# Moving the matmul operands of a three-block transformer kernel to other SBUF addresses

## The chip, the cores and the metric

The kernel runs on one core of one Trainium2 chip. The metric is the device time of one execution in microseconds; a change is judged by the median of several runs against the median of the kernel before on the same chip.

## The reference, cut to what matters

Three transformer blocks are computed one behind the other for 256 tokens of width 1024, all in float32. Block A mixes with dilated band attention in three head groups, block B with ordinary causal attention, block C with a forgetting attention beside a convolution and a pooling branch. Each block ends in a gated MLP of hidden width 2816:

```
x = x + mixer(rmsnorm(x)) @ w_o          # A, B, C: three kinds of mixer
u = rmsnorm(x) @ w_up                     # 1024 -> 2 x 2816
gate, val = split(causal_conv3(u))
x = x + (silu(gate) * val) @ w_down       # 2816 -> 1024
```

## The kernel before, in words

Activations lie transposed, 128 channels on the partitions and 256 tokens along the row. The weights stream from HBM in chunks of 128 x 1024 values through a ring of six buffers `w_raw`. A float32 product is made of three products of a faster float type (`fp32r`): every operand is split into a high part and a low rest, and hi·hi, hi·lo and lo·hi are added in PSUM. ScalarE makes the high part of a weight chunk (`w_hi`), VectorE the rest (`w_lo`); the same is done for the activations (`xg` with a high and a low half for each 128 channels, the attention result `mix_hi`/`mix_lo`, the gated product `g_hi`/`g_lo`).

TensorE runs one list of matmuls in the order of the code, and four patterns make up nearly all of its time. Every matmul is preceded by the load of its 128 x 128 stationary tile, which runs beside the matmul ahead of it.

- **Up-projection pair** (`project2_k`, L417 and L419, 352 pairs in each of the three MLPs): stationary `w_hi`, moving 512 columns (high and low half of `xg` together); then stationary `w_lo`, moving the 256 columns of the high half.
- **Down-projection triple** (L1747 to L1749, 176 triples in each MLP): stationary `w_hi` with `g_hi` moving, `w_hi` with `g_lo`, `w_lo` with `g_hi`, 256 columns each.
- **Out-projection triple** (`out_pe`, L1223 to L1225, 64 triples in each block): the same three with `mix_hi` and `mix_lo`. Block C's six extra projections (L403 to L405, 48 triples) do the same with `xg`.
- **QKV triple** (L665 to L667, 556 triples over the three blocks, and 60 more matmuls of the same shape in L599): here `xg` is stationary and 384 columns of weights move: `w_hi` past the high half of x, `w_lo` past the high half, `w_hi` past the low half.

The SBUF tensors are laid one behind the other in the order in which they are made. The rest of this text speaks of an operand's **residue**: its start address in bytes modulo 128. All steps between the tiles of one tensor (512, 1024, 2048 bytes) are multiples of 128, so that a tensor's tiles have one residue. Two small dummy tensors and three tables set them:

```python
SHIFT = 32
X_AT = (0, 0, 0, 8, 0, 16)              # floats; attention A, MLP A, attention B, MLP B, ...
G_AT = ((0, 0), (8, 8), (24, 24))       # MLP A, B, C: g_hi, g_lo; the tensor starts at residue 32
MIX_AT = ((0, 0), (8, 8), (16, 16))     # attention A, B, C: mix_hi, mix_lo
...
    sb("w_gap", [P, 16])
    w_lo = [sb(f"w_lo{s}", [P, CHUNK], F32R) for s in range(RING)]
    sb("x_gap", [P, 16])
```

```python
    def project2_k(eng, c, e, b, k):
        s = c % RING
        nc.tensor.matmul(bank(b, 0, 2 * TOK), w_hi[s][:, k * P:(k + 1) * P], xg[e][:, k, :, :].rearrange("p h t -> p (h t)"),
                         start=(k == 0), stop=False, skip_group_check=True)
        last = nc.tensor.matmul(bank(b), w_lo[s][:, k * P:(k + 1) * P], xg_hi[e][:, k, :], start=False,
                                stop=(k == KT - 1), skip_group_check=True)
```

The second argument of `matmul` is the stationary tile, the third the moving one.

Of the kernel before, what the change touches and what calls it, by code (L numbers as in the profile page):

```python
# [8 lines left out]
P = 128  # L9
D = 1024  # L10
TOK = 256
KT = D // P
# [27 lines left out]
WARM_UP = 16  # L40
HALVES = 3
GAINS = 16
X0 = 224
GAP = 184
SHIFT = 32
X_AT = (0, 0, 0, 8, 0, 16)
G_AT = ((0, 0), (8, 8), (24, 24))
MIX_AT = ((0, 0), (8, 8), (16, 16))
CHUNK = KT * P
UNIT = 3 * P  # L50
QCHUNK = 2 * UNIT
# [112 lines left out]
def build(nc, x_d, xa_d, stream_d, par_d, con_d, taps_d, out_d):  # L164
    F32 = mybir.dt.float32
    F32R = mybir.dt.float32r
# [5 lines left out]
    def sb(name, shape, dt=F32):  # L172
        return nc.alloc_sbuf_tensor(name, shape, dt)

    def sem(name):
# [2 lines left out]

    w_raw = [sb(f"w_raw{s}", [P, CHUNK]) for s in range(RING)]
    w_hi = [sb(f"w_hi{s}", [P, CHUNK], F32R) for s in range(RING)]  # L180
    sb("w_gap", [P, 16])
    w_lo = [sb(f"w_lo{s}", [P, CHUNK], F32R) for s in range(RING)]
    sb("x_gap", [P, 16])
    x_all = sb("x_all", [P, X0 + KT * TOK])
    xT = x_all[:, X0:X0 + KT * TOK].rearrange("p (k t) -> p k t", t=TOK)
    xg_all = sb("xg", [P, KT * 2 * TOK + SHIFT], F32R)
    xg = [xg_all[:, o:o + KT * 2 * TOK].rearrange("p (k h t) -> p k h t", h=2, t=TOK) for o in X_AT]
    xg_hi, xg_lo = [x[:, :, 0, :] for x in xg], [x[:, :, 1, :] for x in xg]
    mix_all = [sb(f"mix_{n}", [P, KT * TOK + SHIFT], F32R) for n in ("hi", "lo")]
    mix_hi, mix_lo = [[mix_all[n][:, o[n]:o[n] + KT * TOK].rearrange("p (k t) -> p k t", t=TOK) for o in MIX_AT]  # L190
                      for n in range(2)]
    par = sb("par", [P, N_PAR])
    con = sb("con", [P, N_CON])
    zero = sb("zero", [P, TOK], BF16)
    sb("gap", [P, GAP - 3 * SHIFT])
    ln_x = sb("ln_x", [P, TOK])
    rms_r = sb("rms_r", [P, TOK])

# [30 lines left out]
    g_all = sb("g_hi0", [P, 4 * TOK + SHIFT], F32R)  # L229
    g_hi, g_lo = [[[g_all[:, o[n] + (2 * n + b) * TOK:o[n] + (2 * n + b + 1) * TOK] for b in range(2)] for o in G_AT]  # L230
                  for n in range(2)]
# [219 lines left out]
    def norm_gain(e, m):  # L451

        g = PAR_NORM + KT * e + m
        return x_all[:, X0 - GAINS + m:X0 - GAINS + m + 1] if e == 0 else par[:, g:g + 1]

# [1640 lines left out]
    with nc.Block() as block:  # L2096

        @block.sync
        def _(sp):
# [9 lines left out]
            def load_x(m, n, landed):  # L2109
                a, b = GAINS + m * TOK if m else 0, GAINS + (m + n) * TOK  # L2110
                sp.dma_start(x_all[:, X0 - GAINS + a:X0 - GAINS + b], xa_d[:, a:b]).then_inc(landed, 16)

# [297 lines left out]
```

## Time and profile before

| | us |
|---|---|
| median of 3 runs (1051.97 to 1052.17) | 1052.13 |
| the profiled execution | 1052.06 |
| its span, first to last instruction | 1050.2 |
| TensorE busy in it | 1045.3 |
| VectorE, ScalarE, GpSimd busy | 864.6, 686.9, 346.6 |

The 1.9 us between the execution and its span lie around the program. TensorE's matmuls overlap (the drain of one lies over the start of the next), so the length that the trace gives to one matmul is not what it costs; that is the step from its start to the start of the next, which is read from a list of instructions in order of time. Divided over many steps, its 0.01 us of resolution is enough.

### The profile page before, as it was taken

What the parts mean: (1) busy time and instruction counts of PE and PEld (TensorE: products, weight loads), DVE (VectorE), ACT (ScalarE), POOL (GpSimd) and SP (SyncE); (2) the same over time, 40 slices, a digit from 0 to 9 for tenths busy, and PEclk for the clock granted to TensorE, in tenths of its full rate; (3) what the DMA queues carried; (4) which work ended last, traced back from release to release, by engine and by line L of the source; (5) the groups of instructions that cost most, each with busy time, mean ns of one, the idle gap of its engine ahead of it and who ended that gap; (6) DMA issues with size and microseconds to landing.
All of it is one profiled execution on the core that took longest, in us unless ns stands there. A gap on an engine that the chain in (4) does not pass through costs nothing.

```text
span 1050.2 us, 21191 instructions
## 1 busy us (share of the span) xinstructions
PE 1045.3 (100%) x7496; PEld 974.4 (93%) x7496; DVE 864.6 (82%) x1589; ACT 686.9 (65%) x1264; POOL 346.6 (33%) x370
## 2 busy tenths in 40 slices
PE   9999999999999999999999999999999999999998
PEld 8999999999999999999989899999998998999998
DVE  7877778777799888887776999888896769998886
ACT  7766776766766555576776766555686667666563
POOL 4312222112355333332121564333341015653331
PEclk9999999999999999999999999999999999999999
DMA  8644455456466555535453666555433436665541
GB/s 312 235 159 152 156 162 169 149 170 205 159 218 216 189 183 195 166 101 185 152 181 122 200 205 200 192 184 181 153 114 135 161 121 201 209 210 183 196 161 41
DMA packets 57749, 183.34 MB, mean 175 GB/s; under 512 B 6352, under 2 KB 9680, under 8 KB 57424
## 3 DMA queue, kind: packets, MB, share of 16 engines
q1 hardware_dynamic: 56816, 181.52, 52.1%
q10 hardware_dynamic: 864, 0.92, 0.3%
q8 instruction: 41, 0.67, 0.2%
q14 instruction: 28, 0.23, 0.1%
HBM read 181.36 MB, written 1.05 MB: 174 GB/s over the span
## 4 chain that ended last, share of the span: by engine, by line
PE 99%; DMA 0%; DVE 0%; ACT 0%; DVEq 0%; issue 0%
PE ps L417 23%; PE ps L419 12%; PE ps L665 10%; PE ps L667 9%; PE ps L666 9%; PE ps L1747 6%; PE ps L1749 6%; PE ps L1748 6%; PE ps L1223 2%; PE ps L1225 2%; PE ps L1224 2%; PE ps L599 1%; PE ps L843 1%; PE ps L888 1%; PE ps L817 1%; PE ps L855 1%
## 5 line engine op out<-in xcount | busy, mean ns | idle before, releaser
L385 DVE TENSOR_TENSOR w_lo<-w_raw,w_hi 128x1024 fp32r<-128x1024 f32 (+2 forms) x369 | 442.4, 1214 | 45.8 <-ACT w_hi L377 45.5
L377 ACT ACTIVATE w_hi<-w_raw 128x1024 fp32r<-128x1024 f32 (+2 forms) x369 | 353.7, 972 | 150.2 <-PE ps L419 125.2
L417 PE MATMUL ps<-xg,w_hi 128*128 128x512 f32 x1056 | 369.6, 393 | 0.0
L419 PE MATMUL ps<-xg,w_lo 128*128 128x256 f32 x1056 | 294.6, 279 | 0.0
L417 PEld LDWEIGHTS ps<-xg,w_hi 128*128 128x128 f32 x1056 | 198.4, 188 | 41.7 <-DVE xg L482 0.2
L419 PEld LDWEIGHTS ps<-xg,w_lo 128*128 128x128 f32 x1056 | 198.9, 188 | 0.1
L1869 POOL TENSOR_TENSOR prob_t<-prob_t,qkT 128x256 f32<-128x256 f32 x63 | 102.1, 1621 | 279.1 <-ACT prob_t L1792 279.1
L665 PE MATMUL ps<-w_hi,xg 128*128 128x384 f32 (+1 forms) x556 | 193.4, 348 | 0.0
L667 PE MATMUL ps<-w_hi,xg 128*128 128x384 f32 (+1 forms) x556 | 187.6, 337 | 0.0
L666 PE MATMUL ps<-w_lo,xg 128*128 128x384 f32 (+1 forms) x556 | 186.6, 336 | 0.0
L1749 PE MATMUL ps<-g_hi,w_lo 128*128 128x256 f32 x528 | 148.2, 281 | 0.0
L1747 PE MATMUL ps<-g_hi,w_hi 128*128 128x256 f32 x528 | 147.6, 279 | 0.0
L1748 PE MATMUL ps<-g_hi,w_hi 128*128 128x256 f32 x528 | 147.1, 279 | 0.0
L1863 POOL TENSOR_TENSOR qkT<-prob,rms_r 128x256 f32<-128x256 f32 x132 | 121.2, 937 | 18.7 <-DVE prob L1806 13.5
L1839 DVE SCALAR_TENSOR_TENSOR qkT<-qkT,par 128x255 f32<-128x255 f32 (+1 forms) x264 | 111.8, 475 | 5.3 <-ACT qkT L1785 5.2
L665 PEld LDWEIGHTS ps<-w_hi,xg 128*128 128x128 f32 x556 | 104.6, 188 | 3.3 <-issue 2.7
L1785 ACT ACTIVATE qkT<-qkT,par 128x256 f32<-128x256 f32 x132 | 77.6, 597 | 42.4 <-POOL qkT L1863 41.5
L666 PEld LDWEIGHTS ps<-w_lo,xg 128*128 128x128 f32 x556 | 104.5, 188 | 0.1
L667 PEld LDWEIGHTS ps<-w_hi,xg 128*128 128x128 f32 x556 | 104.3, 188 | 0.0
L1747 PEld LDWEIGHTS ps<-g_hi,w_hi 128*128 128x128 f32 x528 | 99.8, 189 | 3.1 <-issue 0.8
L1748 PEld LDWEIGHTS ps<-g_hi,w_hi 128*128 128x128 f32 x528 | 99.1, 188 | 0.0
L1749 PEld LDWEIGHTS ps<-g_hi,w_lo 128*128 128x128 f32 x528 | 99.0, 188 | 0.0
(191 smaller groups left out, 1385.8 us busy)
## 6 DMA issues: line engine op xcount, KB each, us to landing
w_raw<-w_stream SPq DMA_DIRECT2D x228, 512.0 KB, 3.6
w_raw<-w_stream SPq DMA_DIRECT2D x137, 384.0 KB, 3.3
w_raw<-w_stream SPq DMA_DIRECT2D x4, 392.0 KB, 3.0
con<-consts SPq DMA_DIRECT2D x1, 1024.0 KB, 7.6
x_all<-x_t SPq DMA_DIRECT2D x4, 256.0 KB, 5.3
conv_taps<-taps SPq DMA_DIRECT2D x1, 1024.0 KB, 7.4
w_raw<-w_stream SPq DMA_DIRECT2D x4, 192.0 KB, 4.6
x_all<-x_a SPq DMA_DIRECT2D x3, 256.0 KB, 5.7
```

The lines of the kernel that those rows point to most:

```text
L377: nc.scalar.activation(w_hi[s][:, 0:w], w_raw[s][:, 0:w], ACT.Copy).then_inc(w_hi_done, 1)
L385: nc.vector.tensor_tensor(w_lo[s][:, 0:w], w_raw[s][:, 0:w], w_hi[s][:, 0:w].bitcast(F32), ALU.subtract).then_inc(w_lo_done, 1)
L417: nc.tensor.matmul(bank(b, 0, 2 * TOK), w_hi[s][:, k * P:(k + 1) * P], xg[e][:, k, :, :].rearrange("p h t -> p (h t)"), start=(k == 0), st ...
L419: last = nc.tensor.matmul(bank(b), w_lo[s][:, k * P:(k + 1) * P], xg_hi[e][:, k, :], start=False, stop=(k == KT - 1), skip_group_check=True)
L665: nc.tensor.matmul(out, hi, wh, start=(k == 0), stop=False)
L666: nc.tensor.matmul(out, hi, wl, start=False, stop=False)
L667: last = nc.tensor.matmul(out, lo, wh, start=False, stop=(k == KT - 1))
L1747: nc.tensor.matmul(acc(m), wh, g_hi[f][b], start=first, stop=False, skip_group_check=True)
L1748: nc.tensor.matmul(acc(m), wh, g_lo[f][b], start=False, stop=False, skip_group_check=True)
L1749: last = nc.tensor.matmul(acc(m), wl, g_hi[f][b], start=False, stop=True, skip_group_check=True)
L1839: nc.vector.scalar_tensor_tensor(cv_s[b][s][:, k:TOK], up_s[b][s][:, 0:TOK - k], par_col(f, t, per, i, 4 * s + 2 - k), cv_s[b][s][:, k:TOK ...
L1863: nc.gpsimd.tensor_tensor(up_s[t % 2][s], up_sum[s], rms_r[:], ALU.mult).then_inc(F.up, 1)
```

## The change

Only addresses change: no instruction is added, removed or moved on any engine, and no wait. The two dummy tensors go, so that `w_lo` starts at a multiple of 128 bytes as `w_hi` does. X0 grows by as many floats as they had, so that x itself stays where it was. The three tables get other offsets, `mix_hi` and `mix_lo` become 32 floats longer, and a dummy behind them gets shorter by as much, so that all that follows stays where it was; the parameters and constants between move by 256 bytes.

```diff
-X0 = 224
+X0 = 256
-X_AT = (0, 0, 0, 8, 0, 16)
-G_AT = ((0, 0), (8, 8), (24, 24))
-MIX_AT = ((0, 0), (8, 8), (16, 16))
+X_AT = (24, 16, 8, 24, 24, 8)
+G_AT = ((8, 8), (0, 0), (0, 0))
+MIX_AT = ((48, 48), (16, 16), (56, 56))
...
-    sb("w_gap", [P, 16])
-    sb("x_gap", [P, 16])
-    mix_all = [sb(f"mix_{n}", [P, KT * TOK + SHIFT], F32R) for n in ("hi", "lo")]
+    mix_all = [sb(f"mix_{n}", [P, KT * TOK + 2 * SHIFT], F32R) for n in ("hi", "lo")]
-    sb("gap", [P, GAP - 3 * SHIFT])
+    sb("gap", [P, GAP - 5 * SHIFT])
```

The residues that follow, in bytes modulo 128, in the order of blocks A, B, C:

| operand | before | after |
|---|---|---|
| `w_hi` | 0 | 0 |
| `w_lo` | 64 | 0 |
| `xg` in attention | 0, 0, 0 | 96, 32, 96 |
| `xg` in the MLP | 0, 32, 64 | 64, 96, 32 |
| `g_hi`, `g_lo` | 32, 64, 0 | 64, 32, 32 |
| `mix_hi`, `mix_lo` | 0, 32, 64 | 64, 64, 96 |

## Rows read from the trace of the kernel before

**Rows 1.** The page: span, busy time of the engines, chain that ended last

```profile
span 1050.2 us, 21191 instructions
...
PE 1045.3 (100%) x7496; PEld 974.4 (93%) x7496; DVE 864.6 (82%) x1589; ACT 686.9 (65%) x1264; POOL 346.6 (33%) x370
...
PE 99%; DMA 0%; DVE 0%; ACT 0%; DVEq 0%; issue 0%
```

**Rows 2.** MLPs A, B, C: length, busy by engine, granted clock, DMA share, GB/s

```profile
276.79:461.76 184.97, 184.96 (x1236) 170.44 (x1235) 165.32 (x235) 114.31 (x172) 76.43 (x69) 1.00 0.55 184
575.69:761.98 186.29, 186.29 (x1236) 170.52 (x1235) 166.09 (x234) 114.99 (x171) 76.88 (x70) 1.00 0.56 186
863.97:1050.20 186.23, 183.03 (x1236) 168.14 (x1234) 165.13 (x235) 109.08 (x162) 79.41 (x70) 1.00 0.51 169
```

**Rows 3.** TensorE in order of time: up-projection pairs; start us, length us, line

```profile
350.03 0.39 PE L417 MATMUL ps<-xg,w_hi 128*128 128x512 f32 x1
...
352.45 0.39 PE L417 MATMUL ps<-xg,w_hi 128*128 128x512 f32 x1
...
639.82 0.40 PE L417 MATMUL ps<-xg,w_hi 128*128 128x512 f32 x1
...
643.31 0.39 PE L417 MATMUL ps<-xg,w_hi 128*128 128x512 f32 x1
...
950.83 0.39 PE L417 MATMUL ps<-xg,w_hi 128*128 128x512 f32 x1
...
952.53 0.39 PE L417 MATMUL ps<-xg,w_hi 128*128 128x512 f32 x1
...
870.55 0.40 PE L417 MATMUL ps<-xg,w_hi 128*128 128x512 f32 x1
...
874.40 0.40 PE L417 MATMUL ps<-xg,w_hi 128*128 128x512 f32 x1
```

**Rows 4.** The same list: first down-projection matmul, and the pair that follows

```profile
352.80 0.28 PE L1747 MATMUL ps<-g_hi,w_hi 128*128 128x256 f32 x1
...
355.63 0.39 PE L417 MATMUL ps<-xg,w_hi 128*128 128x512 f32 x1
...
643.65 0.28 PE L1747 MATMUL ps<-g_hi,w_hi 128*128 128x256 f32 x1
...
646.49 0.40 PE L417 MATMUL ps<-xg,w_hi 128*128 128x512 f32 x1
...
949.78 0.28 PE L1747 MATMUL ps<-g_hi,w_hi 128*128 128x256 f32 x1
...
950.48 0.40 PE L417 MATMUL ps<-xg,w_hi 128*128 128x512 f32 x1
```

**Rows 5.** The same list: out-projections of blocks A, B, C, second matmul of triples

```profile
254.22 0.28 PE L1224 MATMUL ps<-mix_lo,w_hi 128*128 128x256 f32 x1
...
260.87 0.28 PE L1224 MATMUL ps<-mix_lo,w_hi 128*128 128x256 f32 x1
...
559.90 0.28 PE L1224 MATMUL ps<-mix_lo,w_hi 128*128 128x256 f32 x1
...
565.24 0.28 PE L1224 MATMUL ps<-mix_lo,w_hi 128*128 128x256 f32 x1
...
848.55 0.28 PE L1224 MATMUL ps<-mix_lo,w_hi 128*128 128x256 f32 x1
...
853.75 0.28 PE L1224 MATMUL ps<-mix_lo,w_hi 128*128 128x256 f32 x1
```

**Rows 6.** The same list: QKV triples of block A, and the first chunks (L599)

```profile
132.04 0.34 PE L665 MATMUL ps<-w_hi,xg 128*128 128x384 f32 x1
...
135.17 0.34 PE L665 MATMUL ps<-w_hi,xg 128*128 128x384 f32 x1
...
7.20 1.20 PE L599 MATMUL ps<-w_hi,xg 128*128 128x384 f32 x6
8.24 0.50 PE L599 MATMUL ps<-w_lo,xg 128*128 128x384 f32 x2
```

## Prediction, on record before the changed kernel ran

> **What bounds the kernel now.** I read the page first. TensorE is busy for 1045.3 of 1050.2 us and holds 99% of the chain that ended last [rows 1], so time is won or lost only where a matmul starts earlier or later after the one ahead of it. The granted clock is 1.00 in all three MLPs [rows 2], that is 2.4 GHz, so a slower clock is not the reserve. VectorE, the next engine, is busy for 165 to 166 us of the 185 to 186 us of an MLP [rows 2]: some 19 us of slack in each.
>
> Then I compared the three MLPs with each other. They run the same 1236 matmuls and differ in little but addresses: TensorE is busy in them for 184.96, 186.29 and 183.03 us [rows 2]. The spread of 3.3 us is what addresses (and a few waits) are worth in one MLP, and it has a place: the step from matmul to matmul.
>
> - A pair of the up-projection, 512 + 256 = 768 columns, takes 2.42 us / 7 = 345.7 ns in MLP A, 3.49 / 10 = 349 ns in B, and 1.70 / 5 = 340 ns in C; but at its beginning C runs pairs of 3.85 / 11 = 350 ns on the very same addresses [rows 3].
> - A triple of the down-projection, also 768 columns, takes 2.83 / 8 = 354 ns in A, 2.84 / 8 = 355 ns in B, 0.70 / 2 = 350 ns in C [rows 4].
> - A triple of the out-projection takes 6.65 / 19 = 350 ns in block A, 5.34 / 15 = 356 ns in B, 5.20 / 15 = 346.7 ns in C [rows 5].
> - A QKV triple (1152 columns) takes 3.13 / 6 = 521.7 ns [rows 6].
>
> The best, 340 ns for 768 columns, is 0.443 ns a column; I call that the floor (a QKV triple: 510 ns). What lies above it is the reserve that addresses may hold: per pair 6, 9 and about 2 ns (C's mix of its two rhythms, taken as 342), per down triple 14, 15 and 10, per out triple 10, 16 and 7, per QKV triple 12. With 352 pairs, 176 down triples and 64 out triples a block, and 556 QKV triples, that is 17 x 0.352 + 39 x 0.176 + 33 x 0.064 + 12 x 0.556 = 6.0 + 6.9 + 2.1 + 6.7 = 21.7 us in all.
>
> **A reading of the rows.** While one matmul streams its moving tile, the stationary tile of the next is read. I call the **distance** the residue of the moving tile minus that of the stationary tile being loaded. Before, `w_lo` stood 64 off `w_hi`, so the distance alternated: pairs 64, 0 in A, 96, 32 in B, 0, 64 in C; down triples 32, 96, 32 in A, 64, 0, 64 in B, 0, 64, 0 in C; out triples 0, 64, 0 in A, 32, 96, 32 in B, 64, 0, 64 in C; QKV 0, 64, 0. Odd multiples of 32 are slow where they occur (B's pairs 349, B's out triples 356, A's down triples 354), but the pattern 64, 0, 64 gives 355 in one place and 346.7 in another, and C's pairs show two rhythms. So residues set what is possible, and the rhythm that the engine falls into decides some 8 to 10 ns of it. That is the uncertainty of all that follows.
>
> After the change the distance is constant in every pattern: pairs 64, 96, 32; down triples 64, 32, 32; out triples 64, 64, 96; QKV 32, 96, 32. The trace has one long enough run of constant distance: the six L599 matmuls on `w_hi` (distance 0) take 1.04 / 6 = 173.3 ns each, 520 a triple against 521.7 with the alternating distance [rows 6]. Against the floor of 510 that is 10 instead of 11.7 ns, 15% of the excess gone. No row shows a constant distance of 32, 64 or 96.
>
> **The change part by part**, on the profiled execution of 1052.06 us (the median of the runs is 0.07 above it).
>
> 1. *Pairs.* A's x moves to C's present residue, 64: I give it C's mix, 342 ns, −3.7 ns x 352 = −1.3 us. B (96) and C (32) have no row; I give them the mean of the four measured rhythms, (345.7 + 349 + 340 + 350) / 4 = 346.2: B −2.8 ns, −1.0 us, C +4.2 ns, +1.5 us. Sum −0.8. Bounds: all at 340 is −17 x 0.352 = −6.0; all at 350 is (4.3 + 1 + 8) x 0.352 = +4.7.
> 2. *Down triples.* The mean of the six measured triples is 352; with 15% of the 12 ns of excess gone, 350: −4, −5 and 0 ns x 176 = −1.6 us. Bounds: all at 340 −6.9, all at 356 (2 + 1 + 6) x 0.176 = +1.6.
> 3. *Out triples.* A and B go to 64, where C stands now: 346.7, −3.3 and −9.3 ns; C goes to 96, between 346.7 and 356: 351, +4.3. Sum −8.3 x 0.064 = −0.5 us, between −2.1 and +1.0 (all at 356). The 48 triples of L403 to L405 I leave at zero: 9 ns, the spread of the out triples, would be 0.4 us either way.
> 4. *QKV triples.* The constant run's 520: −1.7 ns x 556 = −0.9 us. Lower bound the floor, −6.5 (11.7 ns). Upper bound: out triples have 16 ns of excess at odd distances against 10 at even ones; the same ratio makes 11.7 ns to 18.7, +7 x 0.556 = +3.9.
> 5. *The other engines.* VectorE writes `w_lo`, and VectorE and ScalarE write `xg`, `g` and `mix` at other residues; the weights land where they did. I put this at nothing: a slower subtraction is covered by the 19 us of slack per MLP, and would cost only above it. The chain has no visible share of VectorE or ScalarE [rows 1]. A shorter or longer step on TensorE also doesn't move the weight stream much: its DMA engines are busy for 51 to 56% [rows 2].
>
> Sum: −0.8 − 1.6 − 0.5 − 0.9 = −3.8 us, **1048.3 us**.
>
> **Rivals.**
>
> *Slower: odd distances are the bad ones.* Nearly all new positions are 32 or 96 away: two of three MLPs in pairs and down triples, C's out-projection, all QKV. In the rows B's pairs and out triples, at 32 and 96, are the slowest of their kind, and A's down triples are slower than C's. Price: pairs at the slow rhythm of 350 +4.7; down triples of B and C at 356 +1.2; out C +0.6 and A, B −0.8; QKV +3.9: +9.6, 1061.7 us. It begins to decide where QKV alone goes up by more than 7 ns a triple, since that eats the whole forecast. With half of it the time is about 1057. Against it: before, 32 and 96 came mixed, and constant they have no row.
>
> *No change, 1052.1 us.* Either TensorE's two reads do not meet, or gains and losses cancel (A's pairs −1.3 against C's +1.5 shows how easily). For the first half speaks nothing in the rows: the same matmuls take 183.03 to 186.29 us [rows 2]. On this the Trainium skill (SBUF — State Buffer, Who interferes with whom) says that TensorE has independent read ports for the moving tile and for the load of the stationary one and never waits on anyone; by that rule residues would be worth nothing and the time would stay at 1052.1, which the three MLPs' spread contradicts unless something else causes it.
>
> *A large gain.* If a constant distance lets the engine fall into the 340 rhythm everywhere, as C's MLP does for most of its pairs, all 21.7 us go: 1030.4. For it: C's pairs hold that rhythm through whole chunks [rows 3]. Against it: the one constant run stays 10 ns above the floor [rows 6]. Half of it is 1041.
>
> **How the numbers follow.** A measurement of this kernel tells about 0.2% (2.1 us) from no change. Forecast, between 1040 and 1050: 0.40. Large gain, below 1040: 0.08. No change, 1050 to 1054.2: 0.20. Slower: 0.32, of which a third, 0.10, above 1058. So faster 0.48, same 0.20, slower 0.32, and the range 1040 to 1058 leaves 0.18 out. Since cases of both signs hold most of the chance: the forecast's own range is 1040 to 1050.
>
> **What would show it.** Same counts of matmuls and a granted clock of 1.00 on both sides; TensorE busy about 183, 184 and 184 us in the three MLPs; pairs near 342 ns in MLP A and 346 in B and C; down triples near 350; QKV triples near 520, out triples of A and B near 347. The forecast is wrong if QKV triples rise above 525, if pairs settle at 350 in two MLPs, or if VectorE's subtraction for `w_lo` gets so much longer that waits for it appear in the chain.

## The result: slower by 0.23%

The changed kernel took 1054.51 us (median of 10 runs, 1054.29 to 1055.85) against 1052.14 us of the kernel before on the same chip: a ratio of 1.0023, 95% interval 1.0014 to 1.0032. The forecast was 1048.3 us in a range of its own from 1040 to 1050. The time lies outside that, on the other side of no change, and still within the wider 1040 to 1058; by the limits of the prediction it is a slower kernel (above 1054.2), which had a chance of 0.32.

The same lines of the page as in [rows 1] (span, busy time of the engines, chain):

```profile
span 1052.6 us, 21191 instructions
...
PE 1047.9 (100%) x7496; PEld 975.5 (93%) x7496; DVE 863.6 (82%) x1589; ACT 686.3 (65%) x1264; POOL 345.2 (33%) x370
...
PE 99%; DMA 0%; DVE 0%; ACT 0%; DVEq 0%; issue 0%
```

The count of instructions and the chain are the same, and TensorE is busy for 2.6 us longer (1047.9 against 1045.3). VectorE takes 1 us less. So the time was lost where the forecast looked for a gain, in the steps of TensorE. The three MLPs, after the change (from and to, length, busy time of TensorE, weight loads, VectorE, ScalarE, GpSimd; granted clock, DMA share, GB/s), beside [rows 2]:

```profile
275.82:462.67 186.85, 186.85 (x1236) 170.80 (x1235) 165.02 (x235) 113.86 (x172) 76.37 (x69) 1.00 0.56 182
576.01:761.99 185.98, 185.98 (x1237) 170.01 (x1235) 166.24 (x234) 115.05 (x171) 77.18 (x70) 1.00 0.58 186
864.81:1052.57 187.76, 184.51 (x1236) 170.11 (x1234) 164.28 (x235) 108.83 (x162) 77.64 (x69) 1.00 0.52 168
```

TensorE's busy time went from 184.96 to 186.85 us in A, from 186.29 to 185.98 in B and from 183.03 to 184.51 in C: +1.9, −0.3, +1.5. The granted clock is 1.00 in all of them, the 2.4 GHz of before.

What a pair and a down triple cost after the change is read from one chunk of each MLP: start of 16 pairs, start of the 8 triples behind them, start of the next pairs (start us, length us, line; L415 is what L417 was, L1745 what L1747 was). They answer to [rows 3, 4]:

```profile
312.80 0.40 PE L415 MATMUL ps<-xg,w_hi 128*128 128x512 f32 x1
...
318.46 0.28 PE L1745 MATMUL ps<-g_hi,w_hi 128*128 128x256 f32 x1
...
321.28 0.40 PE L415 MATMUL ps<-xg,w_hi 128*128 128x512 f32 x1
...
613.08 0.39 PE L415 MATMUL ps<-xg,w_hi 128*128 128x512 f32 x1
...
618.68 0.28 PE L1745 MATMUL ps<-g_hi,w_hi 128*128 128x256 f32 x1
...
621.51 0.39 PE L415 MATMUL ps<-xg,w_hi 128*128 128x512 f32 x1
...
901.70 0.39 PE L415 MATMUL ps<-xg,w_hi 128*128 128x512 f32 x1
...
907.25 0.28 PE L1745 MATMUL ps<-g_hi,w_hi 128*128 128x256 f32 x1
...
910.05 0.39 PE L415 MATMUL ps<-xg,w_hi 128*128 128x512 f32 x1
```

A pair takes 5.66 / 16 = 354 ns in A, 5.60 / 16 = 350 in B, 5.55 / 16 = 347 in C; a down triple 2.82 / 8 = 352.5, 2.83 / 8 = 354 and 2.80 / 8 = 350 ns. The out-projections of blocks A, B and C (first matmul of triples 18, 14 and 14 steps apart), as in [rows 5], and QKV triples of block A, 14 steps apart, as in [rows 6]:

```profile
253.38 0.28 PE L1221 MATMUL ps<-mix_hi,w_hi 128*128 128x256 f32 x1
...
259.74 0.28 PE L1221 MATMUL ps<-mix_hi,w_hi 128*128 128x256 f32 x1
...
560.82 0.28 PE L1221 MATMUL ps<-mix_hi,w_hi 128*128 128x256 f32 x1
...
565.58 0.28 PE L1221 MATMUL ps<-mix_hi,w_hi 128*128 128x256 f32 x1
...
849.13 0.28 PE L1221 MATMUL ps<-mix_hi,w_hi 128*128 128x256 f32 x1
...
854.17 0.28 PE L1221 MATMUL ps<-mix_hi,w_hi 128*128 128x256 f32 x1
```

```profile
100.78 0.34 PE L663 MATMUL ps<-w_hi,xg 128*128 128x384 f32 x1
...
108.06 0.34 PE L663 MATMUL ps<-w_hi,xg 128*128 128x384 f32 x1
```

Out triples take 6.36 / 18 = 353 ns in A, 4.76 / 14 = 340 in B and 5.04 / 14 = 360 in C; a QKV triple takes 7.28 / 14 = 520. The 340 of block B does not hold for its whole stage. After a wait it runs differently, 16 triples in 5.65 us, which is 353 ns:

```profile
569.30 0.28 PE L1221 MATMUL ps<-mix_hi,w_hi 128*128 128x256 f32 x1
...
574.95 0.28 PE L1221 MATMUL ps<-mix_hi,w_hi 128*128 128x256 f32 x1
```

From here on a step is given as the mean over its whole stage, worked out from all starts in the trace; steps more than 4.5% above the stage's median, which hold a wait, are left out on both sides (1 or 2 in 100 in pairs and down triples, 9 to 14 in out triples, 12 to 21 in QKV triples, a third in block C's extra projections). Steps in ns, with what each term of the forecast became:

| term | before A, B, C | after A, B, C | forecast us | measured us |
|---|---|---|---|---|
| pairs (352 an MLP) | 346.7, 350.7, 341.9 | 352.5, 350.1, 346.7 | −0.8 | +3.5 |
| down triples (176) | 353.4, 353.9, 350.1 | 353.5, 353.3, 350.0 | −1.6 | −0.1 |
| out triples (64) | 351.7, 355.7, 347.0 | 353.3, 347.0, 359.8 | −0.5 | +0.4 |
| block C's extra projections (48) | 353.7 | 359.6 | 0 | +0.3 |
| QKV triples (556) | 523.5, 523.0, 526.3 | 519.9, 521.9, 524.0 | −0.9 | −1.6 |
| sum | | | −3.8 | +2.5 |

Each measured term is the sum of the step differences times the counts; their sum of +2.5 us stands beside +2.3 us in the spans (1052.57 against 1050.23) and +2.4 us in the medians. So all of the loss is in these steps. The pairs lose 3.5 us, which is more than the whole; the out triples and the extra projections lose 0.7, and the QKV and down triples give back 1.7. Of block C's QKV triples a quarter move 392 columns instead of 384, and take 534 to 535 ns before and after, so the mean of C stands above those of A and B for that reason alone: its triples of 384 columns are at 523.4 and 520.0 ns.

### The profile page after: what moved, and what is told of

It reads as the page before. It is cut to its first block, busy times and chain, and to the rows that moved or that the text cites. A ratio compares the mean times of both kernels' runs of the same rounds, so it can differ in the third digit from the quotient of the medians.

```text
span 1052.6 us, 21191 instructions
## 1 busy us (share of the span) xinstructions
PE 1047.9 (100%) x7496; PEld 975.5 (93%) x7496; DVE 863.6 (82%) x1589; ACT 686.3 (65%) x1264; POOL 345.2 (33%) x370
## 4 chain that ended last, share of the span: by engine, by line
PE 99%; DMA 0%; DVE 0%; ACT 0%; DVEq 0%; issue 0%
PE ps L415 23%; PE ps L417 12%; PE ps L663 10%; PE ps L664 9%; PE ps L665 9%; PE ps L1745 6%; PE ps L1746 6%; PE ps L1747 6%; PE ps L1221 2%; PE ps L1222 2%; PE ps L1223 2%; PE ps L597 1%; PE ps L841 1%; PE ps L886 1%; PE ps L815 1%; PE ps L853 1%
## 5 line engine op out<-in xcount | busy, mean ns | idle before, releaser
L375 ACT ACTIVATE w_hi<-w_raw 128x1024 fp32r<-128x1024 f32 (+2 forms) x369 | 353.9, 972 | 155.9 <-PE ps L417 130.7
L415 PE MATMUL ps<-xg,w_hi 128*128 128x512 f32 x1056 | 372.7, 393 | 0.0
L417 PE MATMUL ps<-xg,w_lo 128*128 128x256 f32 x1056 | 296.6, 281 | 0.0
L415 PEld LDWEIGHTS ps<-xg,w_hi 128*128 128x128 f32 x1056 | 198.2, 188 | 43.0
L417 PEld LDWEIGHTS ps<-xg,w_lo 128*128 128x128 f32 x1056 | 198.6, 188 | 0.1
L1747 PE MATMUL ps<-g_hi,w_lo 128*128 128x256 f32 x528 | 147.5, 279 | 0.0
L1745 PE MATMUL ps<-g_hi,w_hi 128*128 128x256 f32 x528 | 147.5, 279 | 0.0
L1745 PEld LDWEIGHTS ps<-g_hi,w_hi 128*128 128x128 f32 x528 | 99.2, 188 | 3.1 <-issue 0.3
L1747 PEld LDWEIGHTS ps<-g_hi,w_lo 128*128 128x128 f32 x528 | 99.2, 188 | 0.0
```

Source lines behind the costliest of these rows:

```text
L375: nc.scalar.activation(w_hi[s][:, 0:w], w_raw[s][:, 0:w], ACT.Copy).then_inc(w_hi_done, 1)
L1745: nc.tensor.matmul(acc(m), wh, g_hi[f][b], start=first, stop=False, skip_group_check=True)
L1747: last = nc.tensor.matmul(acc(m), wl, g_hi[f][b], start=False, stop=True, skip_group_check=True)
```

## The experiments

Three questions: do addresses alone decide a step, and is it the distance between two tiles that counts; with what period; and what decides between several steps at the same addresses. In the first four expectations, theory D says that the distance modulo 128 decides alone, theory R that it sets bounds and the state in which TensorE enters a chunk decides some 10 ns of it. Residues are given modulo 256 from here on: `w_hi` stands at 128; `w_lo` at 192 before and at 128 after; x at 128 plus four times its table entry.

### Either half of the change alone

`w_lo` moved, x, gated product and mixed heads where they were before (against the changed kernel):

```diff
-X_AT = (24, 16, 8, 24, 24, 8)
-G_AT = ((8, 8), (0, 0), (0, 0))
-MIX_AT = ((48, 48), (16, 16), (56, 56))
+X_AT = (0, 0, 0, 8, 0, 16)
+G_AT = ((0, 0), (8, 8), (24, 24))
+MIX_AT = ((0, 0), (8, 8), (16, 16))
```

> One part of the change alone: the low weights at residue 0, the three tables as before. Theory D (a pattern's step follows from the distances of moving and next stationary tile, taken modulo 128, wherever it stands): QKV at constant distance 0 runs at the 520 ns a triple that the six L599 matmuls of before showed; the pairs of MLP B (distance 32, 32) run at the 346.7 ns that MLP C shows after the change, the pairs of MLP C (64, 64) at the 352.5 ns that MLP A shows after the change; the down triples of B (64) at 353.5. With MLP A at 0, 0 unknown that is about 1052 to 1055 us. Theory R (distances only bound it, the rhythm in which a pattern is entered decides within some 10 ns): the same distances give other steps, by 3 to 10 ns, in at least one of these places.

The other half: `w_lo` left at 192, the tables of the change (against the kernel before; `mix` is longer and `gap` shorter, as in the change):

```diff
-X_AT = (0, 0, 0, 8, 0, 16)
-G_AT = ((0, 0), (8, 8), (24, 24))
-MIX_AT = ((0, 0), (8, 8), (16, 16))
+X_AT = (24, 16, 8, 24, 24, 8)
+G_AT = ((8, 8), (0, 0), (0, 0))
+MIX_AT = ((48, 48), (16, 16), (56, 56))
```

> The other part alone: the low weights stay at residue 64, x, g and mix get the new tables. Theory D: the pairs of MLP A (distances 0, 64) take the 340 to 342 ns of MLP C before, those of MLP C (96, 32) the 349 to 351 of MLP B before; the down triples of MLP A (64, 0, 64) the 354 of MLP B before, those of B and C (32, 96, 32) the 353.5 of MLP A before; the out triples of A and B (64, 0, 64) the 347 of block C before. QKV and MLP B's pairs (32, 96) have no row. Theory R: at least one of these places differs by 3 ns or more.

Moving `w_lo` alone gave 1055.82 us (ratio 1.0031, 1.0018 to 1.0044), the tables alone 1054.44 (1.0019, 1.0010 to 1.0029): each half is a loss, and the halves do not add up. Where theory D had foretold a step in the first kernel, it came within 1 ns (pairs of B 346.7 and of C 351.8, down triples of B 353.2, QKV triples of A 520.1); the time is 0.8 us above its range. In the second the pairs of A and C came too, and the down triples within 1.5 ns (353.9, 355.0 and 352.4), but the out triples of A and B ran at 353.2 and 354.5 ns for the 347 that D had. In the kernel before, `mix_lo` stands 128 bytes away from `mix_hi` modulo 256; in this one both have one residue, which modulo 128 makes no difference. Together with before and after this is a table of two by two for the pairs, whose x moves by +64, +64 and −32 bytes in A, B and C (ns):

| MLP | neither (before) | `w_lo` alone | x alone | both (after) | both, if the effects added up |
|---|---|---|---|---|---|
| A | 346.7 | 348.0 | 340.1 | 352.5 | 341.4 |
| B | 350.7 | 346.7 | 347.1 | 350.1 | 343.1 |
| C | 341.9 | 351.8 | 348.9 | 346.7 | 358.8 |

In MLP A `w_lo` alone leaves a pair about where it was: 16 pairs between the first two of these rows, from the later part of the first kernel's MLP A (start us, length us, line), take 5.55 / 16 = 347 ns. And x alone brings even a little more than the forecast had given to A (342): between the two rows of the second kernel 16 pairs take 5.44 / 16 = 340 ns, the floor.

```profile
380.87 0.39 PE L415 MATMUL ps<-xg,w_hi 128*128 128x512 f32 x1
...
386.42 0.28 PE L1745 MATMUL ps<-g_hi,w_hi 128*128 128x256 f32 x1
```

```profile
306.86 0.39 PE L417 MATMUL ps<-xg,w_hi 128*128 128x512 f32 x1
...
312.30 0.28 PE L1747 MATMUL ps<-g_hi,w_hi 128*128 128x256 f32 x1
```

With the same x and `w_lo` moved as well, it is 354 ns [the changed kernel's chunk above, 312.80 to 318.46]. What counts is x against both weights tiles: x at 192 stands 64 from `w_hi` and 0 from the old `w_lo`, but 64 from both after the change. MLP C of the first kernel has the same two distances of 64, in another MLP, and nearly the same step, 351.8.

### The same addresses in all three blocks

MLP C's place of x and gated product after the change, in all MLPs, x of the attention stages at 224 and mixed heads at 64 in all (against the changed kernel):

```diff
-X_AT = (24, 16, 8, 24, 24, 8)
-G_AT = ((8, 8), (0, 0), (0, 0))
-MIX_AT = ((48, 48), (16, 16), (56, 56))
+X_AT = (24, 8, 24, 8, 24, 8)
+G_AT = ((0, 0), (0, 0), (0, 0))
+MIX_AT = ((16, 16), (16, 16), (16, 16))
```

> The low weights at 0 and the same offsets in all three blocks: x at 32 and g at 32 in every MLP (as MLP C has after the change), x at 96, 32, 96 in attention and mix at 64. Theory D: pairs 346.7 and down triples 350.0 in all three MLPs, out triples alike in all three blocks, some 4 us below the changed kernel (pairs of A 352.5 to 346.7 and of B 350.1 to 346.7: -3.2 us; down triples of A and B -1.2 us; out triples of C -0.8). Theory R: the three MLPs differ by 3 ns or more a pair or a triple though their addresses are the same.

1050.21 us, ratio 0.9977 (0.9968 to 0.9987). The three MLPs have become alike: pairs 346.8, 346.8, 346.8, down triples 350.0, 350.1, 350.0 ns. So the MLPs' differences were the addresses'. The out triples, which theory D had alike too, ran at 347.3, 347.0 and 342.1 ns at the same distance; each of these is a mean of runs at 340 and at 353 ns, as in block B after the change. TensorE's busy time in them:

```profile
276.01:460.50 184.49, 184.45 (x1237) 170.13 (x1235) 165.46 (x235) 114.75 (x172) 76.75 (x70) 1.00 0.58 184
573.70:758.25 184.55, 184.51 (x1237) 170.21 (x1235) 166.38 (x234) 115.53 (x171) 77.17 (x70) 1.00 0.59 188
860.11:1048.80 188.69, 185.09 (x1236) 170.07 (x1234) 165.23 (x235) 109.23 (x162) 78.12 (x70) 1.00 0.52 167
```

### Is the period 128 bytes?

The gated product 128 bytes further on than after the change, the mixed heads' places of A and B exchanged (128 bytes) and C's moved by 128 (against the changed kernel; the tensor grows by 128 bytes):

```diff
-G_AT = ((8, 8), (0, 0), (0, 0))
-MIX_AT = ((48, 48), (16, 16), (56, 56))
+G_AT = ((40, 40), (32, 32), (32, 32))
+MIX_AT = ((16, 16), (48, 48), (24, 24))
```

> The changed kernel with g 128 bytes further in all MLPs, and mix 128 bytes off (192 to 64 in A, 64 to 192 in B, 224 to 96 in C), so that all residues modulo 128 stay and those modulo 256 change. If 128 bytes are the period: down and out triples as in the changed kernel (353.5, 353.3, 350.0; 353.3, 347, 359.8), 1054.5 us. If the period is 256 or more: out triples of A and B change places (A 340 to 347, B 353), down triples move by several ns.

1054.86 us (1.0024, 1.0014 to 1.0033). Modulo 128 nothing had moved, but the steps did: out triples of A and B exchanged their values with their places (353.3 and 347.0 became 347.3 and 353.4), and down triples went from 353.5, 353.3, 350.0 to 341.0, 359.2, 359.7. Eight down triples of MLP A, then of B, each from its first matmul to the next pair:

```profile
310.87 0.28 PE L1745 MATMUL ps<-g_hi,w_hi 128*128 128x256 f32 x1
...
313.59 0.40 PE L415 MATMUL ps<-xg,w_hi 128*128 128x512 f32 x1
...
609.48 0.28 PE L1745 MATMUL ps<-g_hi,w_hi 128*128 128x256 f32 x1
...
612.35 0.40 PE L415 MATMUL ps<-xg,w_hi 128*128 128x512 f32 x1
```

2.72 / 8 = 340 ns and 2.87 / 8 = 359 ns. A period of 128 bytes, on which all of the forecast rests, is wrong for triples. The 341.0 of MLP A does not hold for its first chunk, whose down triples ran at 353 ns until a wait (first triple of the second chunk, 430 ns).

### One distance for all, a common shift, and new distances

Everything at distance 192, at which the kernel ahead had its 340 ns (against the changed kernel; `xg` grows by 128 bytes, so that all behind it shifts by 128):

```diff
+X_AT = (16, 48, 16, 48, 16, 48)
+G_AT = ((8, 8), (8, 8), (8, 8))
+MIX_AT = ((48, 48), (48, 48), (48, 48))
...
-    xg_all = sb("xg", [P, KT * 2 * TOK + SHIFT], F32R)
+    xg_all = sb("xg", [P, KT * 2 * TOK + 2 * SHIFT], F32R)
```

> The changed kernel with every moving tile of the main steps 192 bytes (modulo 256) beyond the weights that are loaded beside it: x at 192 in the three attention stages (there the weights move, 128 - 192 = -64 = 192), x, gated product and mixed heads at 64. Theory P (the distance modulo 256 decides the step): e4 gave 340.0 to 341.0 ns for down triples and 347.3 ns for out triples at this distance, so down triples 340 in all three stages (350.0 in e3), out triples 340 to 347, pairs near 340 as well (346.8 in e3), QKV triples at or below 520: against e3, 3 x 331 pairs x 6.8 ns + 3 x 156 down triples x 10 ns = 6.8 + 4.7 = 11.5 us less, so 1038 us, and 1035 if the QKV triples gain as well. Theory M (the period is 128 bytes and what e4 showed was chance of the entry): distance 192 is distance 64 of the runs so far, pairs 352, down triples 353, out triples 353: 1054 to 1057 us.

Every tile of the kernel with the same addresses in all blocks, 32 bytes further on:

```diff
+    sb("w_gap", [P, 8])
     w_raw = [sb(f"w_raw{s}", [P, CHUNK]) for s in range(RING)]
...
-    sb("gap", [P, GAP - 5 * SHIFT])
+    sb("gap", [P, GAP - 5 * SHIFT - 8])
...
-G_AT = ((0, 0), (0, 0), (0, 0))
+G_AT = ((8, 8), (8, 8), (8, 8))
```

> e3 with every one of these tiles 32 bytes further on: weights, x, normalized x, mixed heads and gated product, so that every distance is that of e3 and every residue is another. Theory P (only the distance counts): the steps of e3 again, pairs 346.8, down triples 350.0, out triples 347.3, 347.0 and 342.1, QKV triples 519.9, 520.2 and 524.1 ns, and 1050.2 us within 0.15%. Theory F (the place of a tile within its 128 or 256 bytes counts, whatever lies beside it): at least one of the groups moves by 3 ns or more in all three stages, some 3 us up or down.

And distances that no kernel had had (against the changed kernel; `xg` and `g` grow by 128 bytes, `gap` shrinks):

```diff
+X_AT = (32, 40, 48, 56, 8, 32)
+G_AT = ((0, 0), (56, 56), (32, 32))
+MIX_AT = ((0, 0), (32, 32), (8, 8))
```

> The changed kernel at distances that no run has had so far, modulo 256: pairs at 160, 224 and 128 in MLP A, B and C; down triples at 128, 96 and 0; out triples at 0, 128 and 32; QKV triples at 128, 64 and 224. Theory P (the distance modulo 256 decides): down triples of MLP B 360 and out triples of attention C 350 to 353 as at the same distances in the runs so far; the others are not known from a run and may be anything from 340 to 360 ns, the same for a pair and a triple at the same distance within 7 ns. In sum 1050 to 1065 us. Theory M (period 128): pairs as at 32, 96 and 0, so 346.8, 350.1 and unknown; down triples of A and C alike, out triples of A and B alike.

At distance 192 throughout the time was 1059.79 us (1.0073, 1.0056 to 1.0090), where theory P had 1038. The down triples were 353.3 in all three MLPs, not 340; pairs 353.4; out triples of A 340.2, of B and C 346.1 and 350.7. So both theories of this run fell: M because the out triples of A are 13 ns off its value, P because the same distance gave 341.0 in one kernel and 353.3 in another.

The common shift left all MLP steps as they were (pairs 346.7 in all three, down triples 350.1, 350.1, 350.0; QKV 519.9, 520.2, 525.7): 1049.08 us, ratio 0.9971 (0.9961 to 0.9982). So in the MLPs it is the distance that counts, not the place. Out triples moved at the same distance, 347.3 to 340.9 in A and 342.1 to 346.2 in C, as more or fewer of them ran at 340 instead of 353 ns; what two values at one distance mean is asked below. QKV triples of C moved by 1.6 ns (524.1 in the kernel before the shift).

The new distances took 1059.95 us (1.0075, 1.0058 to 1.0091); the two steps that could be foretold came (down triples of B 359.4 for 360, out triples of C 351.7 for 350 to 353). That a pair and a triple at one distance agree within 7 ns, as theory P had it, did not come true: at 96 they take 350 and 359 ns. With it there is a table of mean steps in ns by distance modulo 256, over all kernels above in which both weights tiles stand at the same residue:

| distance | pair | down triple | out triple |
|---|---|---|---|
| 0 | 348.0 | 359.0 | 359.6 |
| 32 | 346.7 to 346.8 | 350.0 to 353.3 | 351.7 |
| 64 | 351.8 to 352.9 | 353.2 to 353.5 | 353.3 to 353.4 |
| 96 | 350.1 to 350.5 | 359.4 | 359.8 |
| 128 | 350.4 | 355.7 to 357.7 | 356.0 to 356.1 |
| 160 | 347.0 | 359.2 to 359.7 | 352.7 |
| 192 | 353.3 to 353.4 | 341.0 or 353.3 | 340.2 to 350.7 |
| 224 | 352.3 | | 354.9 |

Pairs, which move 512 columns at a time, show the same within 2.5 ns at a distance and 128 bytes beyond it; triples do not, their steps differ by up to 13 ns.

### Two steps at one distance

Against the kernel with the same addresses everywhere: gated product at distance 192 in A and B, behind pairs at 32 and at 64; in C it moves by 256 bytes (`g` grows by 128 bytes):

```diff
-X_AT = (24, 8, 24, 8, 24, 8)
-G_AT = ((0, 0), (0, 0), (0, 0))
+X_AT = (24, 8, 24, 16, 24, 8)
+G_AT = ((40, 40), (40, 40), (64, 64))
```

> e3 with three edits. MLP A: gated product 160 bytes further on, so that down triples stand at distance 192 behind pairs at 32. MLP B: x at 192 and the gated product as in A, so down triples at 192 behind pairs at 64, the row of MLP A in e4. MLP C: gated product 256 bytes further on, all else as in e3. Theory E (at distance 192 a step has two values, 340 and 353 ns, and what ran before it picks the one): down triples of B 341.0 as in e4, those of A either 340 or 353 through the whole stage, never the 350.0 of e3; pairs of B 352. Theory P alone (distance decides): A and B alike. For MLP C: if the distance counts modulo 256, down triples 350.0 as in e3; if the period is longer, another value. The time against e3 (1050.2 us): A -1.6 or +0.5, B pairs 331 x 5.5 ns = +1.8 and down triples 156 x 9 ns = -1.4, C 0: 1049 to 1051 us.

1052.21 us (1.0001, 0.9991 to 1.0011), 1.2 us above the range. Its ten runs lie in two groups, four from 1050.97 to 1051.35 us, the profiled one among them, and six from 1052.19 to 1052.98; no trace shows the second group. Pairs of B take 353.2 ns. Down triples of C stayed at 350.1 (350.0): 256 bytes change nothing in them. Those of B are at 340.4. Those of A are at 353.1 in every chunk but one: the second, whose first triple follows a wait. That chunk (from its second triple, 7 steps), the next chunk of A (8), and one of B (8):

```profile
302.28 0.28 PE L1745 MATMUL ps<-g_hi,w_hi 128*128 128x256 f32 x1
...
304.66 0.39 PE L415 MATMUL ps<-xg,w_hi 128*128 128x512 f32 x1
...
310.22 0.28 PE L1745 MATMUL ps<-g_hi,w_hi 128*128 128x256 f32 x1
...
313.05 0.39 PE L415 MATMUL ps<-xg,w_hi 128*128 128x512 f32 x1
...
608.68 0.28 PE L1745 MATMUL ps<-g_hi,w_hi 128*128 128x256 f32 x1
...
611.40 0.40 PE L415 MATMUL ps<-xg,w_hi 128*128 128x512 f32 x1
```

2.38 / 7 = 340 ns, 2.83 / 8 = 354, 2.72 / 8 = 340. Same code and same addresses in the first two, and two steps: at this distance TensorE holds one of two rhythms, and what ran before the chunk picks it. Pairs at 32 (here) or at 192 (the kernel with one distance for all) lead into the slow one, a wait into the fast one here, and pairs at 64 into the fast one, or leave it as it is: MLP A of the kernel with 128 bytes more began slow behind pairs at 64, and was fast from the wait on to its end.

Two steps at one distance are not particular to 192. At distance 32 the down triples are at 350.0 ns, in the mean of a stage, behind pairs at 32, and at 353.2 to 353.3 behind pairs at 0 or 96. And some of the means above hide an alternation: before the change MLP B's pairs settle at 349 and 353 ns in turn, chunk by chunk, and with `w_lo` alone moved MLP C's down triples at 355 and 360. The two buffers of the gated product and the PSUM banks of the up-projection take turns in the same way; no run tells whether they, or what ran before, make this alternation.

### The addresses of before's MLP C, everywhere

Against the kernel before:

```diff
-X_AT = (0, 0, 0, 8, 0, 16)
-G_AT = ((0, 0), (8, 8), (24, 24))
-MIX_AT = ((0, 0), (8, 8), (16, 16))
+X_AT = (0, 16, 0, 16, 0, 16)
+G_AT = ((24, 24), (24, 24), (24, 24))
+MIX_AT = ((16, 16), (16, 16), (16, 16))
```

> The kernel before with the addresses of its own MLP C and attention C in all three: x at 192 in the MLPs, gated product at 0, mixed heads at 64 modulo 256, low weights 64 bytes from the high ones as they were. Theory D (addresses decide, wherever in the program): pairs 341.9 in all three MLPs (346.7 and 350.7 in A and B before), or the 340.1 that MLP A of e2 showed with the same x; down triples 350.1 (353.4 and 353.9 before); out triples near the 347.0 of attention C. Against before: pairs 331 x (4.8 + 8.8) ns = -4.5 us, down triples 156 x (3.3 + 3.8) ns = -1.1 us, out triples 58 x 4.7 + 56 x 8.7 ns = -0.8 us: 1046 us. Theory E (what ran before a step counts as much as its addresses): at least one of A and B keeps a value more than 5 ns away from C's.

As in the kernel before, the place 64 is that of `mix_hi`; `mix_lo` lies at 192 in this kernel and in the three that follow.

The same, with the second matmul of a pair on the high weights, so that the up-projections leave out the product with the low weights:

```diff
-        last = nc.tensor.matmul(bank(b), w_lo[s][:, k * P:(k + 1) * P], xg_hi[e][:, k, :], start=False,
+        last = nc.tensor.matmul(bank(b), w_hi[s][:, k * P:(k + 1) * P], xg_hi[e][:, k, :], start=False,
```

> e9, but the second matmul of a pair loads its weights from the high weights' tile instead of the low one, 64 bytes nearer modulo 128: nothing else changes, and the MLPs' up-projections so leave out the low weights. x at 192 then stands at distance 64 to every tile that a pair loads, as in MLP A of the changed kernel, while buffers, waits and DMAs are those of e9. Theory D (the addresses that TensorE reads side by side decide): pairs 352 ns as there (352.5) and in MLP C of e1 (351.8), against the 341.0 to 341.9 of e9: 3 x 331 x 10.5 ns = +10.4 us, 1056 us. Theory W (what mattered was where the low weights' buffer lies for those who write it, VectorE and the DMA queues): pairs stay at 341 to 342, 1046 us.

The first took 1046.04 us, ratio 0.9945 (0.9928 to 0.9961), for 1046 expected: pairs 341.0, 341.9, 341.9, down triples 350.5, 350.1, 350.5. The second took 1057.21 us (1.0047, 1.0029 to 1.0065), for 1056 expected: pairs 353.2, 352.7, 352.6. TensorE's busy time in the MLPs, first kernel, then second:

```profile
276.61:459.41 182.80, 182.44 (x1236) 168.09 (x1235) 165.99 (x235) 114.68 (x172) 78.00 (x70) 1.00 0.56 186
572.89:755.83 182.94, 182.92 (x1236) 168.25 (x1235) 167.16 (x234) 115.33 (x171) 78.76 (x70) 1.00 0.58 189
857.86:1044.23 186.37, 183.13 (x1236) 168.23 (x1234) 165.07 (x235) 109.09 (x162) 79.43 (x70) 1.00 0.51 169
```

```profile
276.96:463.46 186.50, 186.50 (x1237) 170.49 (x1235) 164.95 (x235) 113.90 (x172) 76.36 (x70) 1.00 0.55 182
576.92:763.55 186.63, 186.63 (x1236) 170.45 (x1235) 166.08 (x234) 114.93 (x171) 77.30 (x70) 1.00 0.56 186
865.57:1055.42 189.85, 186.65 (x1236) 170.35 (x1234) 163.82 (x235) 108.73 (x162) 76.63 (x70) 1.00 0.50 166
```

In the program nothing but the address from which TensorE loads one stationary tile in two differs, and 3.5 to 4.1 us an MLP go with it. The loads lengthen too, from some 168 to some 170.4 us an MLP, which does not tell cause from effect. VectorE and the DMA queues, which write `w_lo`, have no part in it: they write the same addresses in both. What else differs is that the same tile is loaded twice in a row, and with other values; but MLP A after the change has two different tiles at the same distance of 64, and takes 352.5 ns. Together with the table of two by two, in which x decides what a move of `w_lo` is worth, this shows that the address of the moving tile and that of the stationary one act on the step together.

### A further step

Other places for gated product and attention's x, and then the best of them (against the kernel above with before's MLP C everywhere; in the first `g` grows by 128 bytes):

```diff
+X_AT = (16, 16, 8, 16, 32, 16)
+G_AT = ((16, 16), (40, 40), (32, 32))
```

> e9 with the up-projections as they are and new places for the rest: gated product at 224, 64 and 32 (distances to high and low weights 96 and 32, 192 and 128, 160 and 96), x of the three attention stages at 192, 160 and 0 (distances of the moving weights 192 and 0, 224 and 32, 128 and 192). Theory D: pairs stay at 341 to 342 in all three MLPs, since none of their addresses moves. The rest has no run before it with low weights at 192: a down triple may be anything between the 340 and 360 ns seen so far (350.1 to 350.5 in e9), a QKV triple between 515 and 530 (523.4 in e9). If one place gives 340 in a down triple it is worth 156 x 10 ns = 1.6 us in each MLP; in sum 1041 to 1052 us.

```diff
+X_AT = (16, 16, 16, 16, 16, 16)
+G_AT = ((24, 24), (24, 24), (24, 24))
```

> e9 with x at 192 in the three attention stages too, so that each tile has one place in the whole program: x 192, gated product 0, mixed heads 64 modulo 256, low weights where they are before. Theory D: everything of the MLPs as in e9 (pairs 341 to 342, down triples 350), QKV triples of attention A 520.7 as in e11 at the same distances (523.4 in e9), those of B and C near that too (523.1 and 526.2 in e9): 329 x 2.7 + 105 x 2.4 + 52 x 2.4 ns = 1.3 us less than e9, 1044.8 us. Theory E (the entry counts more than the place): QKV triples of B and C keep their values of e9, and the time is 1045.1 or more.

The first took 1047.68 us (0.9965, 0.9952 to 0.9978): pairs 342.0 to 342.5, as expected; down triples 358.7, 354.6, 350.0, none better by more than 0.5 ns than they were; QKV triples 520.7 in A at x = 192, 524.2 and 529.6 at the two other places. The second, x at 192 in all six stages, took 1044.75 us, ratio 0.9933 (0.9919 to 0.9946), for 1044.8 expected, and has the lowest median of all, though its interval overlaps that of the kernel with MLP C's addresses everywhere. Its QKV triples are 520.6 and 521.5 in A and B (523.4 and 523.1), but 526.6 in C (526.2). C's mean holds its triples of 392 columns (537.5 for 534.3 ns); those of 384 columns are at 522.5 (523.3), where theory D has some 520.7 and theory E no change, so C stands nearer to theory E. The page's lines:

```profile
span 1042.9 us, 21191 instructions
...
PE 1037.8 (100%) x7496; PEld 968.1 (93%) x7496; DVE 865.7 (83%) x1589; ACT 687.6 (66%) x1264; POOL 349.5 (34%) x370
```

The same 21191 instructions, and TensorE is busy for 7.5 us less than in [rows 1].

## Why the prediction was wrong

*What bounds the kernel* was right: all of the difference is in TensorE's steps, and addresses are worth several us in them. The reading that the moving tile and the load of a stationary one act on each other was right too: the table of two by two and the kernel whose second matmul reads the high weights show it.

*Pairs* are the step that failed, and in it MLP A: it was given C's mix of 342 ns because its x goes to C's residue. But C's step belonged to x at 192 together with `w_lo` at 192, distances of 64 and 0, and the same change took `w_lo` away from there. The prediction had listed the new distances (64 in A, constant) and then priced A by the residue of x alone. The table of two by two shows the size: x alone 340.1, both 352.5, 11 ns above what the two effects add up to, or 3.9 us in 352 pairs. A came at +2.0 us instead of −1.3, at a step above the 350 that the bounds of this term had as the worst. C's price was right, 346.7 for 346.2; B's mean of four rhythms was 4 ns too low (350.1), +0.8 us.

*Down triples* failed on a second step: 15% of the excess was to go because the distance became constant, from a row of QKV matmuls at distance 0. Constancy as such brings nothing: at constant distances the triples run at anything from 340 to 360 ns. Measured −0.1 for −1.6 us.

*Out triples* failed on the residue modulo 128. A and B were given the same place, and B's mean came as forecast (347.0), but by luck: its triples run at 340 or at 353 ns, none at the steady 347 of block C before. That 347 belonged to `mix_hi` and `mix_lo` 128 bytes apart modulo 256, which the change took away. A, 128 bytes from B modulo 256, stayed at 353.3; exchanging the two exchanged the steps. C at 96 was taken between two rows, 351, and was 359.8. The rows of before could have told it: their down triples of B and out triples of C have the same residue modulo 128 and differ by 8 ns [rows 4, 5], which the prediction put down to the rhythm alone.

*QKV triples* were right in sign and step (519.9 in A for 520); before's mean was 523.7 rather than the 521.7 of [rows 6], since the triples right behind a wait take 529 to 536 ns, so the gain was 1.6 us instead of 0.9. *The other engines* were rightly put at nothing: VectorE is busy for 863.6 us for 864.6.

Of the rivals, "odd distances are the bad ones" had the sign and not the mechanism: the largest loss is at 64, in MLP A's pairs, and QKV, on which it turned, gained. The large gain had as its condition that a constant distance brings 340 everywhere; at constant distances no pair stage came below 346.7. The no-change rival's mechanism is out. On it the Trainium skill (SBUF — State Buffer, Who interferes with whom) has independent read ports for TensorE's moving tile and weight load, and a TensorE that waits on no one; TensorE's 182.44 and 186.50 us in the same MLP, with one stationary address changed, disagree, and the measurement decides.

What stays open: why a distance has the step it has, and why some have two; whether it is the next stationary tile's load that delays the stream or the stream that delays the load; and why the pairs show a period of nearly 128 bytes and the triples do not repeat before 256 (shown for one distance, 32). The runs give a table, not a rule that would foretell a distance that is not in it.

## What to carry to other kernels

Where TensorE bounds a kernel and streams one matmul behind the other, price a moved operand by its distance to every stationary tile that is loaded beside it, never by its own address: two moves that each look good or neutral can spoil each other, and a table of two by two shows it. Before designing a layout, look in the trace for a stage that already runs at the best step and give all stages its whole set of addresses: here that was worth 0.55%, and 0.67% with attention's x, where a new layout of the same tiles cost 0.23%. And a step read from a few rows can be one of two rhythms at the same addresses, so read it over the stage.

## What the runs showed of the hardware

At a granted clock of 1.00, which is 2.4 GHz, three fp32r matmuls of 256 columns took from 340 to 360 ns in kernels that differ in addresses alone: 113.3 to 120 ns each. The distance between the moving and the stationary tile, and what ran before, went with it. A shift of all operands by 32 bytes left the MLPs' steps as they were, and one of the gated product by 256 bytes left the down triples at 350.0. At distance 192 the same triples ran at 340 or at 353 ns through whole chunks, and a wait ahead of one chunk changed its rhythm for that chunk alone in one kernel, and for the rest of the MLP in another.
